# A mixture-of-experts kernel on one Trainium2 core: the down product of the second blocks with the high and low part of h in one operand

## What is computed

```
def hier_moe(x, w_rg, b_rg, w_re, b_re, w_eg, w_eu, w_ed):
    ...                      # top-1 group of 4, then top-2 of its 4 experts: 2 x 1056 token-expert pairs
    def expert_block(args):
        toks, e = args
        xb = x_pad[toks]
        h = jax.nn.silu(xb @ w_eg[e]) * (xb @ w_eu[e])      # 1024 -> 512
        return h @ w_ed[e]                                  # 512 -> 1024
    ...
    y = jnp.zeros((T + 1, D_MODEL), jnp.float32).at[slot_tok].add(out.astype(jnp.float32) * slot_w[:, None])
```

## Time and profile before

| | us |
|---|---|
| median of 3 runs | 1991.69 |
| lowest and highest | 1988.87, 1991.70 |
| profiled execution, its own time | 1985.8 |
| its span, first to last instruction | 1983.7 |
| TensorE busy | 1911.1 (96%) |
| VectorE busy | 1015.7 (51%) |
| ScalarE busy | 753.6 (38%) |
| GpSimd busy | 410.3 (21%) |
| DMA, mean over the span | 163 GB/s |

### The profile page before, as it was taken

The page is one execution under the profiler, slowest core; times in us unless marked ns, Lnnn a source line. Parts: engine busy times, 40 slices in busy tenths (PEclk is TensorE's granted clock), DMA queues, the critical chain, the costliest instruction groups (busy, mean ns, idle before and its releaser), DMA issues. The chain is left out here.

```text
span 1983.7 us, 32313 instructions
## 1 busy us (share of the span) xinstructions
PE 1911.1 (96%) x11976; PEld 1717.4 (87%) x11977; DVE 1015.7 (51%) x1221; ACT 753.6 (38%) x1105; POOL 410.3 (21%) x513
## 2 busy tenths in 40 slices
PE   7999999999999999999999999999999799999995
PEld 5888999999999999889998899888788788887884
DVE  4314355554556565556114431445544666785786
ACT  4322132222244444633112232433321455774674
POOL 2000100000245455551011000000100222242225
PEclk9999999999999999999999999999999899999998
DMA  6121233334244434498434120446125387998997
GB/s 205 63 92 65 75 85 87 94 85 113 81 130 121 142 113 136 127 339 279 148 105 153 54 78 28 159 171 255 35 96 222 118 287 236 367 391 295 314 318 277
DMA packets 224593, 324.33 MB, mean 163 GB/s; under 512 B 15149, under 2 KB 158029, under 8 KB 224449
## 3 DMA queue, kind: packets, MB, share of 16 engines
q1 hardware_dynamic: 189924, 271.96, 40.2%
q0 software_dynamic: 7344, 25.38, 4.9%
q10 hardware_dynamic: 27232, 25.66, 3.7%
HBM read 250.97 MB, written 73.28 MB: 163 GB/s over the span
## 5 line engine op out<-in xcount | busy, mean ns | idle before, releaser
L4157 ACT ACTIVATE e_w_high<-big 128x2048 fp32r<-128x2048 f32 x94 | 175.5, 1910 | 37.7 <-PEq L3704 20.7
L286 PE MATMUL psum<-hT_high,t_w_high 128*128 128x352 f32 x528 | 171.2, 324 | 0.0
L288 PE MATMUL psum<-hT_high,t_w_low 128*128 128x352 f32 x528 | 170.1, 322 | 0.0
L287 PE MATMUL psum<-hT_low,t_w_high 128*128 128x352 f32 x528 | 170.1, 322 | 0.0
L4298 DVE TENSOR_TENSOR e_w_low<-big,e_w_high 128x2048 fp32r<-128x2048 f32 x64 | 143.8, 2288 | 34.8 <-ACT e_w_high L4157 27.4
L286 PE MATMUL psum<-hT_high,scan_w_high 128*128 128x352 f32 x384 | 131.3, 342 | 0.0
L288 PE MATMUL psum<-hT_high,scan_w_low 128*128 128x352 f32 x384 | 124.5, 324 | 0.0
L287 PE MATMUL psum<-hT_low,scan_w_high 128*128 128x352 f32 x384 | 123.8, 322 | 0.0
L4036 PE MATMUL psum<-e_w_high,e_xT 128*128 128x512 f32 x272 | 107.4, 395 | 3.1 <-DVE e_xT L4294 3.0
L4038 PE MATMUL psum<-e_w_high,e_xT 128*128 128x512 f32 x272 | 106.2, 390 | 0.0
L4037 PE MATMUL psum<-e_w_low,e_xT 128*128 128x512 f32 x272 | 106.0, 390 | 0.0
(11 more groups left out here) (623 smaller groups left out, 4970.9 us busy)
## 6 DMA issues: line engine op xcount, KB each, us to landing
big<-in_w_expert_gate SPq DMA_DIRECT2D x32, 1024.0 KB, 7.1
big<-in_w_expert_up SPq DMA_DIRECT2D x32, 1024.0 KB, 10.1
big<-in_w_expert_down SPq DMA_DIRECT2D x32, 1024.0 KB, 12.0
t_w<-in_w_in SPq DMA_DIRECT2D x24, 512.0 KB, 4.7
m_gates<-gate_scr SPq DMA_DIRECT2D x22, 528.0 KB, 4.6
x_scr<-t_conv_out ACTq DMA_DIRECT2D x20, 512.0 KB, 4.8
gate_scr<-s_gate_tanh ACTq DMA_DIRECT2D x16, 528.0 KB, 3.3
scan_w<-in_w_gate SPq DMA_DIRECT2D x16, 512.0 KB, 4.1
```

Of the source, the lines that this page charges most:

```text
L286: nc.tensor.matmul(out, ah, w_h, start=start, stop=False)
L287: nc.tensor.matmul(out, ah, w_l, start=False, stop=False)
L288: return nc.tensor.matmul(out, al, w_h, start=False, stop=stop)
L4157: return nc.scalar.activation(dst, src, ACT.Copy)
```

## The change

It does four things.

1. For blocks of 64 lanes of the experts 1 to 14 the low part of h is put on lanes 64 to 127 of `e_hT_high`, beside the high part on lanes 0 to 63. The new `down_split` does two matmuls for each of the four k and two banks, 16 in place of 24.
2. The result then has its two parts on different partitions. VectorE copies the upper half into `e_out` and adds the lower half (`out_summed`), and ScalarE scales 64 rows of `e_out` in place (`out_split`). Both come after the high and low part of the next h; `out` came before them.
3. The rows of such a block now come out on lanes 0 to 63 and not on the even ones. VectorE makes a table of rows to store to, `e_rows_to`, and changes the weights `tw` in place (`lanes_moved`, once per launch); TensorE brings the even and the odd lanes to the two halves with four small matmuls. GpSimd's third gather comes after its column copies, and its loop waits for the new table.
4. TensorE's loop over the experts takes the first iteration over an expert's blocks of 64 out of the inner loop, since the down product there belongs to the block before, a main one; and behind the main block's gate and up product it branches between `down_split` and `down`.

```diff
@@ VectorE, GpSimd: the tables
+        tab_o = g.sb("e_rows_to", [P, NBLK + 1], U32, ctx=ctx)
+        work = rr[:, 0:NE * (NBLK + 1)].rearrange("p (c e) -> p c e", e=NE)
...
@@ GpSimd
-                nc.gpsimd.tensor_copy(rows[:], tab[:, bass.ds(b, 1)]).then_inc(s_rw, 1)
+                nc.gpsimd.tensor_copy(rows[:], tab_o[:, bass.ds(b, 1)]).then_inc(s_rw, 1)
...
-            for b in range(3):
+            for b in range(2):
                 gather(b)
...
+            gather(2)
+            pool.wait_ge(s_lx, 9)
             nc.gpsimd.tensor_scalar(diag[:], g.ident[:], row_l[:, 0:1], None, ALU.mult).then_inc(s_dg, 1)
+            pool.wait_ge(s_far, MOVED)
@@ TensorE
+            def down_split(b):
+
+                pe.wait_ge(s_hl, b + 1)
+                pe.wait_ge(s_oc, b)
+                for j in range(2):
+                    for k in range(FK):
+                        q, at = GU + k // (FK // 2), (k % (FK // 2)) * D + j * BANK
+                        nc.tensor.matmul(ps[:, DN + j, :], hth[:, k, :], wh[:, q, at:at + BANK], start=(k == 0), stop=False)
+                        mm = nc.tensor.matmul(ps[:, DN + j, :], hth[:, k, :], wl[:, q, at:at + BANK], start=False,
+                                              stop=(k == FK - 1))
...
+            def lanes_moved():
+
+                for src, at in ((m.row[:, 0:NBLK + 1], 0), (m.tw[:, 1:NBLK + 2], NBLK + 1)):
+                    for i in range(2):
+                        mm = nc.tensor.matmul(ps[i * XR:(i + 1) * XR, SPREAD, at:at + NBLK + 1], g.ident[:, i:P:2], src,
+                                              start=True, stop=True)
+                mm.then_inc(s_rt, 1)
...
                 with pe.If(n > 0):
-                    with pe.Fori(0, n) as i:
+                    hidden_split(e, behind + 1)
+                    down(behind)
+                    turn_h(behind + 1)
+                with pe.If(n > 1):
+                    with pe.Fori(1, n) as i:
                         b = within(behind + i)
                         hidden_split(e, b + 1)
-                        down(b)
+                        down_split(b)
                         turn_h(b + 1)
                 b = within(behind + n)
                 hidden(e, b + 1)
-                down(b)
+                with pe.If(n > 0):
+                    down_split(b)
+                with pe.If(n < 1):
+                    down(b)
                 turn_h(b + 1)
@@ ScalarE
+            def out_split(n):
+
+                act.wait_ge(s_ds, n + 1)
+                nc.scalar.activation(ob[0:XR], ob[0:XR], ACT.Copy, scale=m.tw[0:XR, bass.ds(n, 1)]).then_inc(s_oc, 1)
...
+                if split:
+                    with act.If(n < 1):
+                        out(b)
+                        down_parts(e)
+                    h_high(b)
+                    with act.If(n > 0):
+                        out_split(b)
@@ VectorE
             def h_low_split(b):
                 dve.wait_ge(s_hh, b + 1)
-                nc.vector.tensor_tensor(even(htl), ps[:, HT, :].rearrange("p (k t) -> p k t", t=P)[:, :, 0:XR],
-                                        even(hth).bitcast(F32), ALU.subtract).then_inc(s_hl, 1)
+                nc.vector.tensor_tensor(hth[:, :, XR:P], ps[:, HT, :].rearrange("p (k t) -> p k t", t=P)[:, :, 0:XR],
+                                        hth[:, :, 0:XR].bitcast(F32), ALU.subtract).then_inc(s_hl, 1)
+
+            def out_summed(b):
+
+                dve.wait_ge(s_dn, b)
+                dve.wait_ge(s_of, b)
+                nc.vector.tensor_copy(ob[0:XR], flat(ps[XR:P, DN:DN + 2, :])).then_inc(s_da, 1)
+                dve.wait_ge(s_da, b + 1)
+                nc.vector.tensor_tensor(ob[0:XR], ob[0:XR], flat(ps[0:XR, DN:DN + 2, :]), ALU.add).then_inc(s_ds, 1)
...
                 h_low(b)
+                if split:
+                    with dve.If(n > 0):
+                        out_summed(b)
+                    with dve.If(n < 1):
+                        out_whole()
```

More of the change, by code:

```diff
@@ L3808, in stage_experts @@
             "row_last", "row_before", "sample_row_before", "weight_last", "weight_before", "in_both"))
+        tab_o = g.sb("e_rows_to", [P, NBLK + 1], U32, ctx=ctx)
+        work = rr[:, 0:NE * (NBLK + 1)].rearrange("p (c e) -> p c e", e=NE)
+        column, main, inner, moved, firsts, sizes = (r1[:, i * 64:(i + 1) * 64] for i in range(6))
+        moved = r1[:, 512:512 + 2 * (NBLK + 1)]
         diag = g.sb("e_rows_diagonal", [P, P], ctx=ctx)
@@ L3832, in stage_experts @@
         block = ctx.enter_context(nc.Block("experts"))
+        MOVED = 13
         def rows_of(c):
@@ L3857, in expert @@
                         plain(e, i, within(first + i), split, final)
-                last_of(e, n, within(first + n), final)
+                last_of(e, n, within(first + n), split, final)
             expert(0, False, False)
@@ L3944, in _ @@
             before = within(nb - 1)
+            nc.gpsimd.iota(column[:, 0:NBLK + 1], [[1, NBLK + 1]], 0, 0, allow_small_or_imprecise_dtypes=True).then_inc(s_lx, 1)
             pool.wait_ge(s_far, 3)
@@ L4119, in _ @@
             g.keep_busy(UP, 6)
+            lanes_moved()
             hidden(0, 0)
@@ L4245, in plain, with last_of @@
                 turned(b + 1)
-                with act.If(b > 0):
-                    out(b)
-                if not final:
+                if split:
                     with act.If(i < 1):
+                        out(b)
                         down_parts(e)
-                if split:
                     h_high_split(b)
-                else:
+                    with act.If(i > 0):
+                        out_split(b)
+                else:
+                    with act.If(b > 0):
+                        out(b)
+                    if not final:
+                        with act.If(i < 1):
+                            down_parts(e)
                     h_high(b)
-            def last_of(e, n, b, final):
+            def last_of(e, n, b, split, final):
                 silu(b)
@@ L4264, in last_of @@
                     high(e + 1, 3)
-                if not final:
+                if split:
+                    with act.If(n < 1):
+                        out(b)
+                        down_parts(e)
+                    h_high(b)
+                    with act.If(n > 0):
+                        out_split(b)
+                elif not final:
                     with act.If(b > 0):
@@ new lines, in out_whole, with lanes_moved @@
+            def out_whole():
+                dve.sem_inc(s_da, 1)
+                dve.sem_inc(s_ds, 1)
+            def lanes_moved():
+                n = NBLK + 1
+                cols = column[:, 0:n]
+                ch = Chain(dve, s_far, 3)
+                nc.vector.tensor_copy(sizes[:, 0:NE], m.more[:])
+                ch.done(nc.vector.tensor_copy(firsts[:, 0:NE], m.start[:]))
+                ch.done(nc.vector.tensor_tensor(sizes[:, 0:NE], sizes[:, 0:NE], firsts[:, 0:NE], ALU.add))
+                dve.wait_ge(s_lx, 1)
+                ch.done(nc.vector.tensor_tensor(work, last(cols, NE), mid(sizes[:, 0:NE], n), ALU.is_equal))
+                ch.done(nc.vector.tensor_reduce(main[:, 0:n], work, AX, ALU.add))
+                ch.done(nc.vector.tensor_scalar(inner[:, 0:n], cols, firsts[:, 1:2], None, ALU.is_ge))
+                ch.done(nc.vector.scalar_tensor_tensor(inner[:, 0:n], cols, firsts[:, NE - 1:NE], inner[:, 0:n],
+                                                       ALU.is_lt, ALU.mult))
+                ch.done(nc.vector.scalar_tensor_tensor(inner[:, 0:n], main[:, 0:n], 1.0, inner[:, 0:n],
+                                                       ALU.subtract, ALU.mult))
+                dve.wait_ge(s_rt, 1)
+                for src, at in ((m.row[:, 0:n], 0), (m.tw[:, 1:n + 1], n)):
+                    op = nc.vector.tensor_tensor(moved[:, at:at + n], src, ps[:, SPREAD, at:at + n], ALU.subtract)
+                ch.done(op)
+                for at in (0, n):
+                    op = nc.vector.tensor_tensor(moved[:, at:at + n], moved[:, at:at + n], inner[:, 0:n], ALU.mult)
+                ch.done(op)
+                dve.wait_ge(s_lx, 9)
+                nc.vector.tensor_tensor(m.tw[:, 1:n + 1], m.tw[:, 1:n + 1], moved[:, n:2 * n], ALU.add)
+                ch.done(nc.vector.tensor_tensor(tab_o[:], m.row[:, 0:n], moved[:, 0:n], ALU.add))
+                assert ch.base + ch.n == MOVED
@@ L4350, in plain @@
                     h_low_split(b)
+                    with dve.If(i > 0):
+                        out_summed(b)
+                    with dve.If(i < 1):
+                        out_whole()
                 else:
                     h_low(b)
+                    out_whole()
             def last_low():
```

13 lines of the change are left out of this document (8 added, 5 removed).

## The result

The change makes the kernel slower: 2003.39 us (median of 6 runs, 1998.94 to 2009.35) against 1990.28 us for the kernel before in the same series, a ratio of 1.0070, 95% interval 1.0054 to 1.0086. The prediction was 1982.5 us; the time lies 13 us above the top of its range. The profiled execution took 2002.5 us, its span is 2000.3 us, against 1985.8 and 1983.7 before.

A forecast was written before the change was run, and what follows sets the result against it. TensorE was taken as the bound of the expert stage: 10.6 us saved over six blocks, less 1.4 us at expert 9, gives 9.2 us, so the median 1991.69 becomes 1982.5 us; range 1978.5 to 1990.5.

The forecast's parts named there:

- What bounds the kernel: Expert stage: TensorE, busy 96% of the span, is the bound; its savings count fully if nothing else is late.
- Weights: Full DMA stretch from 1682.66 us: it begins earlier when TensorE is earlier, so 5.3 us of experts 1 to 3 stay.
- The rival with the full stretch: Weight loads from 1684 to 1803 us end when they end now, swallowing 5.3 us: 1987.8 us, chance 0.06.
- What is removed: Down products of six second blocks: 16 matmuls in place of 24 save 1.76 us each, 10.6 us in all.
- What is added: VectorE's copy and addition, about 1.2 us each per second block, then ScalarE's scaling: fits with 0.3 us to spare, cost nothing.
- GpSimd's queue: Later store of a second block, gather of x behind it: x lands at 1647.3, needed at 1649.2 us, cost nothing.
- the rival of this name: At experts 1, 2 and 9 the gather behind the store misses by 1.7 us each: 1987.6 us, chance 0.12.
- Expert 9: After its shortened down product TensorE waits for VectorE's x: 1.4 us of the saving lost, between 0 and 1.8.
- Once per launch: VectorE's table of 4.3 us fits its idle time, with GpSimd's copies and TensorE's four matmuls also hidden: cost nothing.
- TensorE's instruction stream: Rival: the longer expert loop with two more compares restarts TensorE, 1.23 us per expert, 17.2 us: 1999.7 us, chance 0.10.
- The signs named for "wrong": TensorE idle time put down to scaling, gather or issue, instruction packets in the loop, or expert 9's gap grown by 5 us.
- The sign for the gather: TensorE idle time before the turn of x, put down to the gather, would show GpSimd's queue late.

The follow-up runs named there:

- e2: Kernel before with TensorE's new loop and 16 matmuls for 24 in second blocks, nothing replacing the 8 left out: 1987.7 us, ratio 0.9993.
- e7: Kernel before with half of each load of down weights left out (5 MB for an expert in place of 6): 1984.82 us, ratio 0.9977.
- e8: e2 with half of each load of down weights left out, as in e7: 1974.17 us, ratio 0.9921 to the kernel before.
- e4: Kernel before, old matmuls, with VectorE's copy and addition into scratch and ScalarE's scaling of second blocks moved behind them: 2004.78 us, ratio 1.0088.
- e6: Changed kernel with ScalarE making the down weights' high parts before the scaling that waits for the tile: 2001.66 us, ratio 1.0061.
- e13: Changed kernel with GpSimd issuing the next gather first and waiting for the store's end just before the next store: 1995.2 us, ratio 1.0033.
- e9: Kernel before with only the once-per-launch table work added, into tiles nobody reads: 1989.03 us, ratio 0.9994.
- e1: Kernel before with only TensorE's new loop and branches, the old 24 matmuls everywhere: 1988.54 us, ratio 0.9995.
- e12: e5 with half of each load of down weights left out, as in e7: 1981.21 us, ratio 0.9956 to the kernel before.
- e5: Changed kernel, ScalarE scaling the upper half early, VectorE adding the lower half in one operation, down weights' high parts ahead of scaling: 1992.62 us, ratio 1.0019.
- e11: e5 with stores that drop lanes without a token: 1983.72 us, ratio 0.9976 to the kernel before.

## Why the prediction was wrong, point by point

**What bounds the kernel: "each microsecond taken from TensorE is a microsecond of the span".** This step failed first. The condition behind it, that the weights are not late, was checked only in one direction: I read from the earlier trace rows that the DMA engines never rest there and from the earlier trace rows that TensorE has only one long wait, and took TensorE as the bound. Both are full at once, and here the work taken from TensorE alone gave almost nothing back. e2 (0.9 us of 10.6) and the pair e7 and e8 (10.7 us) show it.

**Weights: "the whole stretch begins earlier ... and the 5.3 us of three experts are kept".** In e2 the whole stretch lies 2.3 to 2.5 us earlier, less than half of the 5.3. Its start did move with TensorE, as forecast, but the load that opens it (1683.29) precedes expert 3's short product (1684.40), so only two savings lie in front of it, less 1.0 us that the turn before 1658.32 took more. The savings of experts 9, 10 and 12 lie where VectorE and ScalarE are already waiting for loads. In the changed kernel the same load comes 3.6 us later than before (1688.52 - 1590.10 = 98.4 against 94.8). The rival with the full stretch had the mechanism and 0.06 of the chance; it was drawn too small, for experts 1 to 3 only.

**What is removed: 6 x 1.76 us.** Right: 3.73 us a product, 1.8 us less than before, and 1.7 less at expert 9.

**What is added: "so it fits with 0.3 us to spare ... I cost this at nothing".** The sum was right to a tenth, the question too narrow. Counted from the first down product, the result was forecast at 1632.0 us and came at 1634.33 - 2.26 = 1632.07, and TensorE never waited for it. The 0.3 us allowed for the branch and the gaps, an estimate that no row backs, were 0.20 in the timelines after: 0.04 and 0.03 before VectorE's two operations (1630.58 and 1631.84), 0.13 before ScalarE's (1633.18). This step failed second. Something else hangs on when the result is ready: the store, which holds `e_out` until it lands, 9.2 us here, and ScalarE's next `out` needs that tile. Section "The kernel before" says that ScalarE may write the tile only then, and I did not ask when that is. e4 shows the whole loss, 16 us, from the late result alone.

**GpSimd's queue: "cost nothing".** The store's start was forecast at 1632.8 and came at 1635.14 - 2.26 = 1632.9; it landed after 9.2 us, where I took 8.5 and 9.7 as the other end. The gather behind it was in time, as said: in the changed kernel TensorE never waited for x to be gathered. But h was late there before it. Where it is not, in e4 and e6, TensorE does wait for the gather (7.6 and 10.9 us), and in these the rival of this name is right in its mechanism. What failed was to follow the queue for one block only. The lag is handed on from store to store to the last one, 5 us in the last stretch; e13, without it, is 7 us faster in all. The rival looked at x only, not at the last store.

**Expert 9: 1.4 us back.** The mechanism was right and the size nearly so. Behind the shortened product x came last, as forecast (VectorE delivers it at 1820.63 + 1.21 = 1821.84), the next matmul started 1.3 us later (1823.11), and the wait is 1.69 us, where 1.4 was the forecast. What was not foreseen is that the wait before the product grew as well, from 1.9 to 2.5 us, for a low part of h that is later still.

**Once per launch: nothing.** Right (e9).

**TensorE's instruction stream.** Its predicted time, 1999.7 us, is the nearest to the result, but its mechanism is absent: the new loop alone takes 1988.54 us, a ratio of 0.9995 (e1), and neither e1's trace nor the changed kernel's has a packet of an instruction queue between 1640 and 1920 us. A rival that gives the right number is not thereby right. Whether a still longer loop would cost something, no run shows.

**The signs named for "wrong".** I listed idle time put down to the scaling, to the gather, to issue, or at expert 9. In the changed kernel the wait that decided is none of TensorE's: it is ScalarE's own, in the row of L4242. The sign for the gather appears not there but in experiments (e4, e6, e12).

## What to carry to other kernels

Before pricing a saving on the busiest engine, look for a second engine or the DMA share at its limit in the same stretch: where both are full, cut a load in one experiment, with and without the saving, to see which of them the time follows. When a result comes later, list everyone who depends on when its tile becomes free, up to the end of its store, and what stands behind each of them in its queue; moving the first reader's work ahead, or filling the tile early and adding the rest in place, can keep the old handover (e5, with both, gave back some 10 of 13 us). A queue that waits for its store's end before it issues the next load can hand a delay on to the end of the kernel, as here. And when an edit that removes a wait gains little, look in its trace for the wait that took its place (e6).

## What the runs showed that I had not expected

A late operand can cost TensorE more than its lateness. At 1691 us h was 0.8 us late; another 2.1 us passed before the next product, whose x VectorE delivers only behind that h, and it took 2.7 us more at a granted 0.79: 5.6 us for a delay of 0.8. In e2 at 1897.92 it was 1.08, 2.10 and 2.8 us (granted 0.78). The clock does not fall each time: waits of 1.12 and 1.70 us before 1660.35 left the next product of 32 matmuls at 7.65 us, with a granted clock of 1.00. And dropping the empty lanes of the stores, which moves 13% fewer bytes on that queue, was worth 1 to 2 us by itself, hardly more than the runs can tell, and 9 us between e5 and e11 by their medians (ratios 1.0019 and 0.9976, taken in two series). That the change had made stores and loads the bound would explain it; no run shows this apart from the times.
